# Output projection by token tiles, with the second norm and turn behind each tile and the residual added by VectorE

## What is computed

```python
x = x + ga1 * (jnp.concatenate([hy, ret, att], axis=-1) @ p['w_out'])
x = x + ga2 * squared_relu_mlp(modulate(x, p['norm2_g'], sh2, sc2), p['mlp_w1'], p['mlp_w2'])
# modulate(x, gain, shift, scale) = rms_norm(x, gain) * (1 + scale) + shift
```

## Time and profile before

| | us |
|---|---|
| median of 3 runs | 4117.21 |
| lowest, highest | 4112.95, 4119.3 |
| the profiled execution | 4111.42 |
| its span | 4109.6 |
| PE busy | 3657.5 (89%) |
| DVE, ACT, POOL busy | 2192.9 (53%), 1430.1 (35%), 1142.6 (28%) |

### The profile page before, as it was taken

How to read it: one execution, slowest core, us unless ns; L and a number is a source line. 1 busy time by engine, 2 the same in 40 slices (tenths; PEclk the granted TensorE clock), 3 DMA queues, 4 the chain that set the end, 5 groups by cost and what they waited for, 6 DMA issues and landing times. The chain is left out here.

```text
span 4109.6 us, 53361 instructions
## 1 busy us (share of the span) xinstructions
PE 3657.5 (89%) x19724; PEld 3073.2 (75%) x19724; DVE 2192.9 (53%) x3864; ACT 1430.1 (35%) x2818; POOL 1142.6 (28%) x1019
## 2 busy tenths in 40 slices
PE   7979975989777899999999899769897779999998
PEld 3668974777666678888888679758786668888886
DVE  5478345766674344444444583357676534454454
ACT  2331125766522332222222411247673232222222
POOL 1121110111100234455444421101110024454554
PEclk9989987999988999999999899779998889999999
DMA  5345100000224111111101161000004411111111
GB/s 190 127 152 190 49 3 29 8 38 1 102 96 167 36 42 41 41 41 38 33 31 41 67 210 59 4 26 6 37 6 159 148 38 60 41 51 51 41 51 56
DMA packets 154422, 267.88 MB, mean 65 GB/s; under 512 B 9112, under 2 KB 121129, under 8 KB 151818
## 3 DMA queue, kind: packets, MB, share of 16 engines
q1 hardware_dynamic: 147148, 216.31, 16.0%
q0 software_dynamic: 5776, 44.04, 2.7%
q10 hardware_dynamic: 1328, 5.24, 0.3%
...
## 5 line engine op out<-in xcount | busy, mean ns | idle before, releaser
L2641 POOL TENSOR_TENSOR x<-x,mlp_tmp 128x512 f32<-128x512 f32 x576 | 785.2, 1396 | 806.0 <-DVE mlp_tmp L2622 800.9
L2622 DVE TENSOR_TENSOR mlp_tmp<-psum,gate 128x512 f32<-128x512 f32 x576 | 391.6, 688 | 273.3 <-POOL x L2641 194.7
L152 PE MATMUL psum<-act_hi,w_hi 128*128 128x512 f32 (+1 forms) x1280 | 473.0, 370 | 12.6 <-DVE w_lo L2600 12.6
L153 PE MATMUL psum<-act_lo,w_hi 128*128 128x512 f32 (+1 forms) x1280 | 472.5, 369 | 0.0
L154 PE MATMUL psum<-act_hi,w_lo 128*128 128x512 f32 (+1 forms) x1280 | 472.3, 369 | 0.0
L152 PE MATMUL psum<-w_hi,hidden_hi 128*128 128x512 f32 x1152 | 450.0, 391 | 0.0
L153 PE MATMUL psum<-w_lo,hidden_hi 128*128 128x512 f32 x1152 | 448.5, 389 | 0.0
L154 PE MATMUL psum<-w_hi,hidden_lo 128*128 128x512 f32 x1152 | 448.4, 389 | 0.0
L2614 DVE TENSOR_TENSOR hidden_lo<-square,hidden_hi 128x512 fp32r<-128x512 f32 x160 | 102.3, 639 | 592.6 <-ACT hidden_hi L2586 592.6
L2578 ACT ACTIVATE relu<-psum 128x512 f32<-128x512 f32 x160 | 88.9, 555 | 666.6 <-PE psum L154 666.6
L1728 DVE TENSOR_REDUCE att_max<-psum 128x1 f32<-128x512 f32 (+2 forms) x272 | 217.8, 801 | 179.7 <-PE psum L154 179.6
...
## 6 DMA issues: line engine op xcount, KB each, us to landing
w_raw<-in_mlp_w SPq DMA_DIRECT2D x128, 512.0 KB, 3.8
...
```

What stands on the lines that cost most here:

```text
L152: pe.matmul(out, lhs[0], rhs[0], start=start, stop=False)
L153: pe.matmul(out, lhs[0], rhs[1], start=False, stop=False)
L2622: dve.tensor_tensor(tmp[:, j % 2, :], ps[:, 4 + j % 4, :], gate[:, int(t >= LAT_TILES), 512 * h:512 * h + 512], ALU.mult).then_inc(gated.s ...
L2641: pool.tensor_tensor(a, a, tmp[:, j % 2, :], ALU.add).then_inc(added.sem, 1)
```

## The change

- The order of the projection: w_out is taken whole, k in the order 2, 3, 0, 1, 4 to 7 (`OUT_ORDER`). Tiles 0 to 3 with both halves fill all eight banks k by k; then each tile's two units of 24 matmuls follow, in banks 0 to 3.
- Rows 0 and 1 are cast from Hyena's own buffers in SBUF; the write to `cat_dram` and the wait for it are gone. Rows 2, 3 and the weights of k 2 to 5 are loaded before Hyena ends. Raw rows and raw weights lie where their low parts will be, so no ring is left. Of rows 2 to 7, ACT and DVE cast the first 512 tokens ("early") ahead of the rest ("late").
- x is waited for in three parts.
- DVE adds the residual itself (L2533), behind each product (L2530). POOL has nothing in the block.
- The second norm and the turn run inside the block, tile by tile, through banks 4 to 7: behind tile 4's matmuls PE turns tiles 0 and 1, behind tile 5 tiles 2 and 3, behind tile 6 tiles 4 and 5, then one a tile, and two behind the last. ACT applies scale and shift in the bank, in pieces of 128 features by 128 tokens (L2479), and casts (L2485). The separate `turn_x("norm2", ...)` is gone.
- SP issues the first MLP weights when the last unit is done.

```diff
@@ -1910,14 +1910,14 @@
+    ahead = [kit.at("hy_ahead0", [P, 4, 8, 512], 0, F32R), kit.at("hy_ahead1", [P, 1, 8, P], 122, F32R)]
+    behind = [kit.at("hy_back0", [P, 4, 4, 512], 64, F32R), kit.at("hy_back1", [P, 4, 1, P], 126, F32R)]
+    z = [kit.at("hy_z0", [P, 2, SEQ], 96), kit.at("hy_z1", [P, 2, CTX], 120)]
...
+    zth = [kit.at("hy_zT0_hi", [P, 8, W], 160, F32R), kit.at("hy_zT1_hi", [P, 2, W], 128, F32R)]
+    ztl = [kit.at("hy_zT0_lo", [P, 8, W], 168, F32R), kit.at("hy_zT1_lo", [P, 2, W], 130, F32R)]
...
@@ -2025,13 +2023,12 @@
             for step in steps[2:]:
                 spectrum(step)
+            sp.wait_ge(conved.sem, conved[((0, X2), 1)])
+            out_row(kit, l, sp, 3)
             sp.wait_ge(z_done.sem, z_done[steps[-1]])
-            out_first_loads(kit, l, sp)
-            for s in reversed(range(len(lengths))):
-                for ct in range(2):
-                    sp.wait_ge(z_out.sem, z_out[(s, 1, (ct, 1))])
-                    sp.dma_start(kit.cat_dram[ct * P:(ct + 1) * P, col0[s]:col0[s] + lengths[s]], z[s][:, ct, :]).then_inc(out_sent.sem, 16)
-            sp.wait_ge(out_sent.sem, out_sent.total)
+            out_weights(kit, l, sp, 0)
+            out_row(kit, l, sp, 2)
+            out_weights(kit, l, sp, 1)
...
+OUT_ORDER = [2, 3, 0, 1, 4, 5, 6, 7]
+OUT_W = [(2, 4), (4, 6), (0, 2), (6, 8)]
+def out_raw(kit):
+    return (kit.at("w_out_raw", [P, KT, D], 152), kit.at("cat_raw", [P, KT, TOK], 40), kit.at("cat_aside", [P, TOK], 196))
...
+def out_weights(kit, l, q, j):
+    k0, k1 = OUT_W[j]
     w_dram = kit.io["w_out"][l].rearrange("(t p) n -> p t n", p=P)
+    q.dma_start(out_raw(kit)[0][:, k0:k1], w_dram[:, k0:k1]).then_inc(kit.sig(f"out_w{j}", 16).sem, 16)
...
+def out_row(kit, l, q, k):
+    n_tok = TOK if l < DEPTH - 1 else SEQ
+    _, rows, aside = out_raw(kit)
+    to = aside[:, 0:n_tok] if k == 3 else rows[:, k, 0:n_tok]
+    q.dma_start(to, kit.cat_dram[k * P:(k + 1) * P, 0:n_tok]).then_inc(kit.sig(f"out_row{k}", 16).sem, 16)
...
 def phase_out(kit, l):
...
+    FIRST = 4
+    xn = kit.at("out_xn", [P, KT, TOK], 0)
...
+    wh, wl = hl(kit, "w_out", [P, KT, D], 120)
+    gate = kit.at("gate1", [P, 2, D], 184)
+    tmp = kit.at("out_tmp", [P, 2, 512], 192)
...
+    early = [(k, 0) for k in OUT_ORDER]
+    late = [(k, 1) for k in OUT_ORDER if k >= 2]
...
+    turns_after = {4: (0, 1), 5: (2, 3), 6: (4, 5)}
+    for t in range(7, n_tiles):
+        turns_after[t] = (t - 1,) if t < n_tiles - 1 else (t - 1, t)
...
+    def bank(t, h):
+        return ps[:, 2 * t + h if t < FIRST else (2 * t + h) % 4, :]
...
+    def turn_bank(t, i):
+        return ps[:, 4 + 2 * (t % 2) + i, :]
...
+    def part_of(k, late_part):
+        if k < 2:
+            out = [(slice(0, SEQ), z[0][:, k, :])]
+            return out + ([(slice(SEQ, TOK), z[1][:, k, :])] if n_tok > SEQ else [])
+        cols = slice(FIRST * P, n_tok) if late_part else slice(0, FIRST * P)
+        return [(cols, aside[:, cols] if k == 3 else rows[:, k, cols])]
...
+            out_weights(kit, l, sp, 2)
+            out_row(kit, l, sp, 4)
+            out_row(kit, l, sp, 5)
+            out_weights(kit, l, sp, 3)
+            out_row(kit, l, sp, 6)
+            out_row(kit, l, sp, 7)
...
+                if j == 1:
+                    sp.wait_ge(c_lo.sem, c_lo[(1, 0)])
+                sp.dma_start(x[:, t:t + n, :], src.rearrange("(t p) n -> p t n", p=P)).then_inc(x_in[j].sem, 16)
+            sp.wait_ge(c_lo.sem, c_lo[(3, 1)])
+            mlp_gate_loads(kit, l, sp)
+            sp.wait_ge(done.sem, done[units[-1]])
+            mlp_first_loads(kit, l, sp)
...
+            def row_hi(k, late_part):
+                if k >= 2:
+                    act.wait_ge(row_in[k].sem, row_in[k][0])
+                for cols, src in part_of(k, late_part):
+                    last = act.activation(xh[:, k, cols], src, ACT.Copy)
+                last.then_inc(c_hi.sem, 1)
...
+            def weights_hi(k):
+                j = [k0 <= k < k1 for k0, k1 in OUT_W].index(True)
+                act.wait_ge(w_in[j].sem, w_in[j][0])
+                if k == 0:
+                    act.wait_ge(c_lo.sem, c_lo[(1, 0)])
+                act.activation(wh[:, k], w_raw[:, k], ACT.Copy).then_inc(w_hi.sem, 1)
...
+            def square(t):
+                act.wait_ge(added.sem, added[(t, 1)])
+                act.activation(xl[:, :, tokens(t)], x[:, t, :].rearrange("p (b c) -> p b c", c=P), ACT.Square,
+                               accum_out=ss[:, t:t + 1]).then_inc(squared.sem, 1)
+            def roots(t):
+                act.wait_ge(meaned.sem, meaned[t])
+                act.activation(root[:, t:t + 1], ss[:, t:t + 1], ACT.Sqrt).then_inc(rooted.sem, 1)
...
+            def modulate(t):
+                c = int(t >= LAT_TILES)
+                for i in range(2):
+                    act.wait_ge(turned.sem, turned[(t, i)])
+                    for b in range(4):
+                        m = 4 * i + b
+                        o = turn_bank(t, i)[:, b * P:(b + 1) * P]
+                        last = act.activation(o, o, ACT.Identity, scale=kit.factor[:, 1, m, c:c + 1],
+                                              bias=kit.mod[:, 3 * KT + m, c:c + 1])
+                    last.then_inc(modulated.sem, 1)
+                    act.wait_ge(modulated.sem, modulated[(t, i)])
+                    if i == 0:
+                        act.wait_ge(turned.sem, turned[(t, 1)])
+                    act.activation(xh[:, blocks(i), tokens(t)], turn_bank(t, i).rearrange("p (b c) -> p b c", c=P),
+                                   ACT.Copy).then_inc(hi_done.sem, 1)
+            for k in OUT_ORDER:
+                if k == 0:
+                    row_hi(0, 0)
+                    row_hi(1, 0)
+                elif k != 1:
+                    row_hi(k, 0)
+                weights_hi(k)
+            for k, _ in late:
+                row_hi(k, 1)
+            for t in range(FIRST):
+                square(t)
+                roots(t)
+            for t in range(FIRST, n_tiles):
+                for m in turns_after[t]:
+                    if m < t:
+                        modulate(m)
+                square(t)
+                roots(t)
+            modulate(n_tiles - 1)
...
+            def row_lo(k, late_part):
+                dve.wait_ge(c_hi.sem, c_hi[(k, late_part)])
+                for cols, src in part_of(k, late_part):
+                    last = dve.tensor_tensor(xl[:, k, cols], src, xh[:, k, cols].bitcast(F32), ALU.subtract)
+                last.then_inc(c_lo.sem, 1)
...
+            def evict(t):
+                for h in range(2):
+                    a = x[:, t, 512 * h:512 * h + 512]
+                    if t % 4 == 0 and h == 0:
+                        dve.wait_ge(x_in[t // 4].sem, x_in[t // 4][0])
+                    dve.wait_ge(done.sem, done[(t, h)])
+                    if t:
+                        dve.wait_ge(added.sem, added[(t - 1, h)])
+                    dve.tensor_tensor(tmp[:, h, :], bank(t, h), gate[:, int(t >= LAT_TILES), 512 * h:512 * h + 512],
+                                      ALU.mult).then_inc(gated.sem, 1)
+                    dve.wait_ge(gated.sem, gated[(t, h)])
+                    dve.tensor_tensor(a, a, tmp[:, h, :], ALU.add).then_inc(added.sem, 1)
...
+            def norm(t):
+                c = slice(t, t + 1)
+                dve.wait_ge(squared.sem, squared[t])
+                dve.tensor_scalar(ss[:, c], ss[:, c], 1.0 / D, EPS, ALU.mult, ALU.add).then_inc(meaned.sem, 1)
+                dve.wait_ge(rooted.sem, rooted[t])
...
+                link(dve, dve.tensor_tensor(rinv[:, c], rinv[:, c], t1[:, c], ALU.mult))
+                dve.tensor_scalar(xn[:, :, tokens(t)], x[:, t, :].rearrange("p (b c) -> p b c", c=P), rinv[:, c], None,
+                                  ALU.mult).then_inc(scaled.sem, 1)
...
+            def turned_lo(t):
+                for i in range(2):
+                    dve.wait_ge(hi_done.sem, hi_done[(t, i)])
+                    dve.tensor_tensor(xl[:, blocks(i), tokens(t)], turn_bank(t, i).rearrange("p (b c) -> p b c", c=P),
+                                      xh[:, blocks(i), tokens(t)].bitcast(F32), ALU.subtract).then_inc(lo_done.sem, 1)
...
+            for k, _ in late:
+                row_lo(k, 1)
+            dve.wait_ge(gate_in.sem, gate_in[1])
+            for t in range(FIRST):
+                evict(t)
+            for t in range(FIRST):
+                norm(t)
+            for t in range(FIRST, n_tiles):
+                evict(t)
+                if t < n_tiles - 1:
+                    norm(t)
+                for m in turns_after[t]:
+                    if m < t:
+                        turned_lo(m)
+            norm(n_tiles - 1)
+            turned_lo(n_tiles - 1)
...
+            def turn(t):
+                pe.wait_ge(scaled.sem, scaled[t])
+                for i in range(2):
+                    if t < 2:
```

(31 more changed lines are left out.)

162 lines of the change are left out of this document (45 added, 117 removed).

## The result

| | kernel before | changed kernel |
|---|---|---|
| median of the runs, us (lowest to highest) | 4118.26 (4112.95 to 4120.23, 4 runs) | 4043.82 (4039.59 to 4045.88, 4 runs) |
| ratio, 95% interval | 1 | 0.982 (0.9809 to 0.9832) |
| profiled execution, its span, us | 4111.42, 4109.6 | 4045.88, 4044.1 |
| stretch of layer 0, us | 179.5 | 137.6 |
| stretch of layer 1, us | 142.2 | 113.3 |

The forecast was 4053 us, in a range from 4038 to 4080. By the medians the change saves 74.4 us, by the profiled spans 65.5, by the two stretches that it rewrites 70.8. (A stretch runs, as in the prediction, from the end of VectorE's last Hyena product to the end of its last low part before the MLP.) In a second comparison on one chip, with five runs of the changed kernel against nine of the kernel before, the medians stood 70.0 us apart (4114.13 and 4044.17, ratio 0.9831, 0.9818 to 0.9845).

The account below looks back on a forecast made before the run. TensorE, busy 89% of the span, was taken as the bound through its waits between Hyena and MLP. Savings of 39.1 (layer 0) and 26.2 us (layer 1), less 1 us of clock, and 5.8 us to the median gave 4053 us, range 4038 to 4080.

Parts of the forecast that it names:

- start: From Hyena's last VectorE product to the first projection matmul: boundary, casts, subtraction and hand-overs, 3.3 us a layer.
- lower clock at the start: First projection matmuls after TensorE's pause: 12 at the 1.2 GHz level, 0.2 us extra each, 2.4 us a layer.
- turns in the stream: Transposes of tiles between projection matmuls, 1.33 us for eight: 10.6 us in layer 0, 8.0 in layer 1.
- loop wait: First two-tile round of turns: TensorE waits for modulates, square, norm and low parts, 1.0 us; later rounds just fit.
- tail: Behind the last projection matmul: half turns, modulates, square, norm and low part, 14.3 us a layer.
- the modulates: ScalarE's scale and shift in the turn banks, 0.37 us per 128-column operation, four in 1.48 us.
- The clock's two restarts: Slow matmuls at the projection's start, 2.4 us a layer, and at layer 0's MLP start, 1 us.
- the best case's 4038: Lower end of the range; rival with modulates at 0.28 us and no lower clock at the start, chance 0.08.
- these 25 us: Margin for x: loads ahead and with it need 20 us, wanted after some 45; without it 12.8 us return.
- The rounds do fit: Against the rival of slow modulates and strided writes exposing waits each round: gain 34 us, 4083 us, chance 0.20.
- the clock did not stay down: Against the rival that transposes interrupting the projection keep the clock low: 4139 us for half the matmuls; slower, chance 0.03.
- No feed was late: Against the rival that x or w_out's last rows land behind need: 21 us back, 4074 us, chance 0.06.

Follow-up runs that it names:

- first_two: Changed kernel with the projection's first stage over two tiles in place of four: median 4041.4 us, stretches 3.2 us shorter than the changed kernel's.
- before_x_early: Kernel before with gates and x loaded right behind the first two gathered rows: median 4117.5 us, ratio 0.9999 to the kernel before.
- double_cast: Changed kernel with ScalarE copying each turned half tile a second time: median 4057.1 us, stretches 15.0 us longer than the changed kernel's.
- turn_at_once: Changed kernel with layer 0's tiles 7, 8 and 9 turned as soon as projected, not one tile behind: median 4057.6 us, stretches 13.6 us longer.
- turns_last: Changed kernel with all turns behind the last tile's projection: median 4085.4 us, stretches 35.8 us longer than the changed kernel's.

## Why the prediction came out right, step by step

| step, us | layer 0: taken, measured | layer 1: taken, measured |
|---|---|---|
| start | 3.3, 3.28 | 3.3, 3.28 |
| matmuls of the stream | 108.8, 108.8 | 87.0, 87.0 |
| lower clock at the start | 2.4, 2.5 | 2.4, 1.9 |
| turns in the stream | 10.6, 7.9 | 8.0, 6.1 |
| loop wait | 1.0, 1.0 | 1.0, 1.0 |
| tail | 14.3, 14.0 | 14.3, 14.0 |
| stretch | 140.4, 137.6 | 116.0, 113.3 |

The measured clock term is 1272.20 - 1266.94 us for the first 12 matmuls, less 12 at 0.227; the turns are what is left of the stream (120.3 us in layer 0, 96.1 in layer 1).

**Right in mechanism and size.** The start; the loop's wait, its place and its cause; the tail within 0.3; evictions hidden under tile 4 (VectorE's pairs 1.34 us apart, TensorE without a wait there); the strided scaling at no cost (0.75 us, 0.07 more than before's, and covered); the MLP's weights in time; the modulates, taken as 1.48 for four and measured at 1.46 to 1.48. The estimate of 1.64 from the Trainium skill ("ScalarE: Activation LUTs", What ACT_TABLE_LOAD costs) lies above it, so the row of the 128-column kin was the better guide. The clock's two restarts: ten slow matmuls before the MLP of layer 0 after a pause of 7.06 us, six and part of a seventh before after 5.49; that is 0.7 us against 1.0 taken.

**Mis-sized.** The turn. I took 1.33 us for eight transposes from the earlier trace rows, a row that stands alone between waits, with the last transpose's full duration in it. In the stream the next matmul starts before that has ended: 0.99 us a turn, 2.7 us less in layer 0 and 1.9 less in layer 1. These, 0.5 us of clock at layer 1's start and the tails are the 5.5 us by which the stretches gained more (70.8 against 65.3).

**Right in part by luck.** The loop's 1.0 us came out to 0.1 us from terms that were each a little off. ScalarE began 0.06 us behind the turns' end (1325.66 and 1325.60) and not 0.75 ahead, since the fourth root held it; its four halves took 8.0 us (1325.66 to 1333.66) and not 8.4, and TensorE's cover was longer, 1336.77 - 1325.60 = 11.2 and not 10.9. The forecast of the profiled execution came within 1.5 us because the stretches gained 5.5 us more than forecast while the rest of the span was 5.3 us longer, for which the 5.9 us of clock in the retention block are enough. And I added 5.8 us because before's profiled execution lay that far below its median. The changed kernel's profiled execution lay 2.1 above its own. The forecast of that execution was 4047.4, its time 4045.9; the rest of the 9 us between 4053 and 4043.8 is this shift, which belongs to an execution and not to a kernel. The range's lower end is also called the best case's 4038, while the working puts that case at 4042, or 4036 on the profiled execution's scale.

**Wrong in its weight.** "That the feeding hides behind matmuls rests on these 25 us" held as a number (x landed 17.9 us after its issue at 1267.94, 22.7 before its first use at 1308.58), but first_two shows that half of the cover does as well. What the wait for x hung on in the kernel before was more than its place in the queue, as before_x_early shows: rows that came one ring place at a time, a wait for all of x at once, and loads issued only behind the boundary.

**The rivals.** The rounds do fit, yet with little to spare: double_cast is this rival made true, and cost 15.0 us for 0.60 more on each half. In the stream the clock did not stay down, neither here nor with the pauses of 6.9 and 4.9 us of turn_at_once; it did in the uncovered turns of turns_last, where it hardly counts. No feed was late. The change did what it says.
